# Half of the final modulation vector's steps on GpSimd, beside the output projection

## What is computed

```python
def _hybrid_mixer(...):
    ...
    return o @ w_o                      # the output projection

def reference(...):
    c_act = jax.nn.silu(c)
    ...
        x = x + g1 * _hybrid_mixer(h, ...)
        h = _modulate(_rmsnorm(x, norm2_gain[l]), sh2, sc2)
        x = x + g2 * _swiglu(h, w_gate[l], w_up[l], w_down[l])
    sh_f, sc_f = jnp.split(c_act @ w_mod_final + b_mod_final, 2, axis=-1)
    return _modulate(_rmsnorm(x, final_gain), sh_f, sc_f)
```

## Time and profile before

| | us |
|---|---|
| median of 3 runs | 1448.45 (1447.98 to 1451.27) |
| the profiled execution, whole | 1446.68 |
| the profiled execution, span from first to last instruction | 1445.0 |

### The profile page before, as it was taken

One profiled execution on the slowest core, in us unless ns is written; L12 is line 12 of the kernel. 1 busy time (PEld: TensorE's weight loads), 2 busy tenths in 40 slices (PEclk: granted clock), 3 DMA queues, 4 the chain that ended last, 5 costly groups with the idle time before them and its releaser, 6 DMA issues.

```text
span 1445.0 us, 18548 instructions
## 1 busy us (share of the span) xinstructions
PE 1341.7 (93%) x6181; PEld 1071.6 (74%) x6181; DVE 1023.3 (71%) x1468; ACT 684.6 (47%) x1157; POOL 727.8 (50%) x628
## 2 busy tenths in 40 slices
PE   2899999997899999989998899999999999999997
PEld 2668888785566666657876778888888888887886
DVE  4678699987877655554775986666666666378787
ACT  5456677736676655554125633223323334354332
POOL 3135444556677866652002165555555556578552
PEclk9899899998999999998999999999999999999999
DMA  9521234457534343312753244444444435989432
GB/s 326 178 62 30 88 126 135 144 162 203 131 76 114 88 125 116 89 43 84 272 172 114 88 152 155 167 168 167 168 158 146 146 141 197 362 296 327 150 109 117
DMA packets 123562, 220.20 MB, mean 152 GB/s; under 512 B 9386, under 2 KB 52500, under 8 KB 123220
## 3 DMA queue, kind: packets, MB, share of 16 engines
q1 hardware_dynamic: 123476, 219.12, 45.7%
HBM read 160.90 MB, written 57.93 MB: 151 GB/s over the span
## 4 chain that ended last, share of the span: by engine, by line
PE 41%; DVE 7%; issue 2%; DMA 1%; ACT 1%; POOL 0%; DVEq 0%; POOLq 0%; ACTq 0%
PE ps_out L2339 25%; PE ps_out L2365 12%; PE ps_out L1694 1%; DVE mod_acc_final L1759 1%; PE ps_out L1678 1%; DMA scr_mod_final<-mod_acc_final 1%; DVE y_full L1780 1%; DVE wgu_lo L2446 0%; PE ps_out L1702 0%; ACT square_junk L2257 0%; DVE x L2601 0%; DVE y_gated L1792 0%; DVE down_part L2599 0%; DVE h_sum_t L2413 0%; DVE h_t_full L2413 0%
## 5 line engine op out<-in xcount | busy, mean ns | idle before, releaser
L2036 POOL TENSOR_TENSOR wgu_lo<-wgu_raw,wgu_hi 128x512 fp32r<-128x512 f32 x66 | 97.4, 1483 | 127.6 <-ACT wgu_hi L2028 127.6
L2273 POOL TENSOR_TENSOR dn_lo<-dn_raw,dn_hi 128x512 fp32r<-128x512 f32 x77 | 126.9, 1665 | 67.1 <-ACT dn_hi L2179 67.0
L2028 ACT ACTIVATE wgu_hi<-wgu_sum 128x512 fp32r<-128x512 f32 x88 | 55.2, 632 | 199.7 <-DVE wgu_sum L2429 80.0
L2339 PE MATMUL ps_out<-h_b_t_hi,wgu_hi 128*128 128x512 f32 x352 | 138.1, 392 | 6.6 <-DVE h_b_t_lo L2417 2.6
L483 POOL TENSOR_TENSOR win_lo<-win_raw,win_hi 128x256 fp32r<-128x256 f32 (+1 forms) x84 | 66.7, 824 | 141.0 <-ACT win_hi L473 115.7
L2339 PE MATMUL ps_out<-h_b_t_hi,wgu_lo 128*128 128x512 f32 x352 | 137.7, 391 | 0.0
L2339 PE MATMUL ps_out<-h_b_t_lo,wgu_hi 128*128 128x512 f32 x352 | 137.5, 391 | 0.0
L2179 ACT ACTIVATE dn_hi<-dn_raw 128x1024 fp32r<-128x1024 f32 x77 | 81.2, 1062 | 114.4 <-PE ps_out L2365 55.7
L2365 PE MATMUL ps_out<-dn_hi 128*128 128x512 f32 x308 | 120.2, 390 | 0.0
L2365 PE MATMUL ps_out<-dn_hi,dn_lo 128*128 128x512 f32 x308 | 119.8, 389 | 0.0
L2365 PE MATMUL ps_out<-dn_lo,dn_hi 128*128 128x512 f32 x308 | 119.8, 389 | 0.0
(11 more groups left out here) (356 smaller groups left out, 3648.9 us busy)
## 6 DMA issues: line engine op xcount, KB each, us to landing
scr_act_sums<-act_sums SPq DMA_DIRECT2D x11, 1792.0 KB, 6.7
dn_raw<-scr_act_sums SPq DMA_DIRECT2D x77, 256.0 KB, 5.3
wmod_c<-in_w_mod_dram SPq DMA_DIRECT2D x48, 256.0 KB, 2.9
wgu_raw<-in_w_gate_dram SPq DMA_DIRECT2D x11, 1024.0 KB, 5.3
wgu_raw<-in_w_up_dram SPq DMA_DIRECT2D x11, 1024.0 KB, 5.4
wd_sums<-in_w_down_dram SPq DMA_DIRECT2D x11, 1024.0 KB, 4.8
scr_wd_sums<-wd_sums SPq DMA_DIRECT2D x11, 1024.0 KB, 4.1
dn_raw<-scr_wd_sums SPq DMA_DIRECT2D x44, 256.0 KB, 7.0
```

Of the source, the lines that this page charges most:

```text
L2036: pool.tensor_tensor(sl[slot(m, x)][:], src, sh[slot(m, x)][:].bitcast(F32), ALU.subtract).then_inc(wlp, 1)
L2273: pool.tensor_tensor(bl[q % NSLOT][:, 1], braw[entry(q)][:, 1], bh[q % NSLOT][:, 1].bitcast(F32), ALU.subtract).then_inc(dlw, 1)
L2339: last = pe.matmul(bank(m, b), a[s][:, t], h[x][t // 2][:, t % 2], start=(fresh and t == 0 and a is sh and h is hh), stop=(t == 3 and a is ...
```

## The change

The 32 steps are split by column group. VectorE keeps groups 0 and 1, 16 steps, two in each of tiles 0 to 7. GpSimd takes groups 2 and 3, also 16 steps, in a loop of its own between the 1/rms of the head groups (line 1644) and the 1/rms of row blocks 0 to 3 (line 1646). A GpSimd step is one multiplication for the first step of a group, and for the others a multiplication in place in the load buffer, a wait for it, and an addition to its own accumulator `fb`. Each side has two load buffers where there were four, in the same memory, and each has its own semaphores. In SyncE's queue the loads alternate: GpSimd's load of step f, then VectorE's load of step f, each waiting until its own step f - 2 is done. The two waits for all stores of the vector (64 of one semaphore) become waits for 32 of each of two, and one of ScalarE's waits gains a partner.

```diff
-    NFW = 4
+    fb = nc.alloc_sbuf_tensor_at("mod_acc_final_pool", [P, HALF], F32, offset=g.top - 14 * 1024)
+    NFW = 2
     fw = nc.alloc_sbuf_tensor_at("wmod_final", [P, NFW, HALF], F32, offset=g.top - 8 * 1024)
+    fx = nc.alloc_sbuf_tensor_at("wmod_final_pool", [P, NFW, HALF], F32, offset=g.top - 4 * 1024)
...
-    NF, FY = 4 * KD, 8
+    NF, FY = 2 * KD, 8
...
+        def load_final_pool(f):
+            c, t = f // KD, f % KD
+            if f >= NFW:
+                sp.wait_ge(fpa, f - NFW + 1)
+            if f >= KD and t == NFW - 1:
+                sp.dma_start(modf[:, half(2 + c - 1)], fb[:]).then_inc(fpo, 16)
+            sp.dma_start(fx[:, f % NFW], A["w_mod_final"][P * t:P * t + P, half(2 + c)]).then_inc(fxl[f % NFW], 16)
+
         for n in range(NY):
             for f in final_steps(n):
+                load_final_pool(f)
                 load_final(f)
             if n == FY:
                 sp.wait_ge(fmd, NF)
-                sp.dma_start(modf[:, half(3)], fa[:]).then_inc(fmo, 16)
+                sp.dma_start(modf[:, half(1)], fa[:]).then_inc(fmo, 16)
+                sp.wait_ge(fpa, NF)
+                sp.dma_start(modf[:, half(3)], fb[:]).then_inc(fpo, 16)
...
         pool.tensor_tensor(rc[:, NT:2 * NT], rc[:, NT:2 * NT], g.nhalf[:], ALU.pow).then_inc(rsd, 1)
+        for f in range(NF):
+            c, t = f // KD, f % KD
+            pool.wait_ge(fxl[f % NFW], 16 * (f // NFW + 1))
+            by = g.csil[:, t:t + 1].to_broadcast([P, HALF])
+            if t == 0:
+                if c:
+                    pool.wait_ge(fpo, 16 * c)
+                pool.tensor_tensor(fb[:], fx[:, f % NFW], by, ALU.mult).then_inc(fpa, 1)
+            else:
+                pool.tensor_tensor(fx[:, f % NFW], fx[:, f % NFW], by, ALU.mult).then_inc(fpr, 1)
+                pool.wait_ge(fpa, f)
+                pool.wait_ge(fpr, f - c)
+                pool.tensor_tensor(fb[:], fb[:], fx[:, f % NFW], ALU.add).then_inc(fpa, 1)
         pool.wait_ge(s2, 4)
...
-            act.wait_ge(p4.fmo, 64)
+            act.wait_ge(p4.fmo, 32)
+            act.wait_ge(p4.fpo, 32)
...
         act.wait_ge(p4.fmd, p4.NF)
+        act.wait_ge(p4.fpa, p4.NF)
```

More of the change, by code:

```diff
@@ L1551, in phase4 @@
     fmo = k.sem("mod_final_stored")
-    NF, FY = 4 * KD, 8
+    fxl = k.sems("wmod_final_pool_loaded", NFW)
+    fpr = k.sem("mod_final_pool_product")
+    fpa = k.sem("mod_final_pool_added")
+    fpo = k.sem("mod_final_pool_stored")
+    NF, FY = 2 * KD, 8
     STEP_T = {(1, 10): 0, (0, 10): 1, (1, 11): 2, (0, 11): 3, (1, 12): 4, (0, 12): 5, (1, 13): 6, (0, 13): 7}
@@ L1802, in phase4 @@
     p.yam, p.yfr, p.ysc, p.x1r, p.s2, p.rs2, p.fmd, p.fmo, p.ybm = yam, yfr, ysc, x1r, s2, rs2, fmd, fmo, ybm
+    p.fpa, p.fpo = fpa, fpo
     p.NY, p.NF = NY, NF
@@ L2139, in sync @@
                 sp.wait_ge(u2n, 4)
-                sp.wait_ge(p4.fmo, 64)
+                sp.wait_ge(p4.fmo, 32)
+                sp.wait_ge(p4.fpo, 32)
                 sp.dma_start(mfin[:], modf.rearrange("p (c n) -> p c n", c=4)).then_inc(mfl, 16)
```

## The result

The changed kernel takes 1451.45 us (median of 20 runs, 1448.7 to 1454.3), the kernel before, run beside it, 1447.77 us (median of 20, 1444.7 to 1451.27). The ratio is 1.0026, with a 95% interval from 1.0018 to 1.0035: 3.7 us slower, 0.26%. The profiled execution of the changed kernel took 1449.02 us with a span of 1447.3, against a span of 1445.0 before.

A forecast was written before the change was run, and what follows sets the result against it. It took the start of early_xhat, following VectorE's pace, to set the rest. A 5.9 us delay less 1.1 us from TensorE gave +4.8 us: 1453.2 us, 0.33% slower, range 1447.8 to 1458.5 for 8 in 10.

The forecast's parts named there:

- The start of early_xhat: VectorE's scaling after tile 7's work, which the feed-forward part hangs on: 756.0, 5.9 us later than 750.1.
- the walk: Working through the 16 projection steps across three engine streams with landings, queue and mutual waits: GpSimd's last step ends at 754.5.
- 4.9 of holding: Projection: VectorE and GpSimd instructions with SBUF operands wait for each other, 4.9 of the 5.9 us on early_xhat.
- 1.0 of loads: Projection: GpSimd's loads through two buffers and SyncE's queue, and the change of group, 1.0 of the 5.9 us.
- The hand-over of 0.14 us: Between VectorE and GpSimd: the waiting engine gets in 0.14 us before the other's running instruction ends.
- Rival 2: Projection: neither engine gets in before the other has quite ended; +11.4 - 1.1, so 1458.8 us; chance 0.08.
- rival 3: Projection: no holding between the engines, only the loads; +1.0 with no change of clock, 1449.4 us; chance 0.15.
- rival 4: Faster: GpSimd's last step ends before 748.7, early_xhat 3.0 us earlier than now, 1445.4 us; chance 0.08.
- rival 5: SyncE's queue starves both sides, loads behind stores land in 4.8 us; +10.3 - 1.1, 1457.7 us; chance 0.09.
- the row: Profile row for SyncE's loads in the projection: 3.8 us to land, the median of 28.
- What TensorE gives back: Around tile 10: longer idling moves the slow clock stretch, so tile 14's y_sb runs faster; -1.1 us, bounds 0 and -1.5.
- the term of the clock: TensorE's granted clock after its idle time ahead of the first transpose: -1.1 us in the sum.

The follow-up runs named there:

- e1: Changed kernel with each GpSimd multiplication and addition of the 16 steps replaced by two fills with zero, loads and waits kept: 1446.73 us, 0.9995 of the kernel before.
- e9: Changed kernel with GpSimd's loads issued by GpSimd itself, load f + 2 right after step f, in place of SyncE: 1454.44 us, 1.0043 of the kernel before.
- e4: Kernel before, all 32 steps on VectorE, with an accumulator for each of the four groups: 1444.1 us, 0.9969 of the kernel before.
- e5: Changed kernel with two accumulators a side, so neither engine waits for its first group's store: 1453.39 us, 1.0038 of the kernel before.
- e7: Changed kernel with two accumulators a side and the 1/rms of row blocks 0 to 3 ahead of GpSimd's steps 14 and 15: 1452.32 us, ratio 1.0035.
- e6: Changed kernel with GpSimd's two 1/rms instructions for row blocks 0 to 3 moved ahead of its steps 14 and 15: 1452.28 us, ratio 1.0038.

## Why the prediction came out as it did

*The start of early_xhat: right.* Forecast 57.2 us after tile 0 (5.9 later than before), measured 57.11 (5.84 later). It ended idle by GpSimd's 1/rms, as said. GpSimd's last step ended 55.69 us after tile 0 (forecast 754.5 - 698.85 = 55.65), VectorE's 54.6 (54.6), the store of GpSimd's first group left at 26.1 (26.6). The way there was off at two places, so the hit within 0.1 us is in part luck. The x addition of tile 7 ended at 49.65, not 51.15, because VectorE trailed less and then stood 2.73 us for its last load. And GpSimd's steps 9 and 11 ended at 33.65 and 40.16, where the walk had 35.15 and 42.15; then the load of step 12 stood in SyncE's queue behind the store of row block 2, which waits for VectorE's x addition of tile 5, and landed 4.75 us after its issue. The walk had given these steps 3.8 us and no such store. The two misses, some 2 us each, cancel: step 13 ended at 49.10 (49.05).

*What it is made of: right in the main.* 4.9 of holding and 1.0 of loads were 4.6 and 1.2 by e1. The means said the same: GpSimd's multiplications 1241 ns and additions 1508, 0.20 and 0.24 above 1.04 and 1.27 where I had said 0.25; steps of VectorE 1368 within 1.1 to 1.4; x additions 1082 and y_gated 895, less than the 1.1 I had given them; y_full 740. The hand-over of 0.14 us held too: the x addition that starts at 745.23 and takes 1.59 waits 0.90, so that it gets in at 746.13, and GpSimd's addition of 744.72 ends at 746.27. Rival 2, full exclusion to the end, falls by this and by its 11.4; rival 3, no holding, falls by these means and by e1; rival 4 needed GpSimd's last step at 748.7 or sooner, 49.85 after tile 0, and it ended at 55.69; rival 5 needed 4.8 us a landing, and the medians are 3.6 and 3.9.

*The loads of SyncE's queue.* At the Trainium skill's fit ("DMA: Bandwidth & Descriptors", section on the anatomy of one DMA), an estimate of 2.6 us for 256 KB, the forecast was +2.6 us and 1451.1. The 13 GpSimd loads issued from 700 to 751 took 3.6 at the median, so the trace decides for the row and not for the fit, which is for GpSimd's queue. In e9, where these loads are on that queue, they took 3.9 at the median too. The time by itself would have misled: 1451.45 is nearer to the 1451.1 than to the 1453.2 of the forecast.

*What TensorE gives back: the step that was mis-sized.* Forecast 1.1 us, bounds 0 and 1.5. Measured 5.84 - 3.97 = 1.87, above the upper bound. The mechanism was as written: 6.57 us idle ahead of the first transpose (6.6), a second wait of 0.77 (under 2), the slow stretch on y_d of tile 10, and y_sb of tile 14 at full clock. But the way from the second transpose to the next y_d went from 5.12 us (759.56 to 764.68) to 3.58 (763.39 to 766.97): 1.54, with the two transposes that I had left to the bound. The other 0.33 lies between early_xhat and that transpose; the kernel before had an idle 0.46 us ahead of its x addition of tile 8, which the changed kernel hasn't.

*The sum.* +4.8 forecast, +3.97 in the traces, +3.7 in the medians, 0.26%; with 20 runs a side the interval (1.0018 to 1.0035) does not reach 1. I had set the bound of what a measurement tells at 0.3% and gave more chance to the side above it (0.53) than below (0.39); the time came out below, by the term of the clock. With 1.87 in its place the sum is +4.0 us, 0.28%.

*What the prediction missed.* Its comparison was of the change with the kernel before. That the gain that VectorE could have, some 5 us, was to be had from the waits for the stores alone, with GpSimd left out of it (e4), was in rows that I had read and summed up as 7.3 us. And my expectations for e5 to e7 all fell: each took a wait away and I let the ones behind it move up, without asking which other wait lay under it.

## What to carry to other kernels

Before work is moved from VectorE to GpSimd, count on both engines the instructions that take two operands from SBUF: each pair that meets can cost each side up to most of the other's running instruction (here an x addition of 0.69 us became 1.59), so that VectorE, with 16 of 32 steps moved away, was busy 3.4 us longer. Look first for what else makes the engine trail; here separate accumulators in place of one that waits for its store brought 3.8 us and no contention. Where a buffer is freed late, several waits lie under each other: price the removal of one by the next one that ends, in the queue's own order.

## What the hardware showed that I had not expected

- A plain fill on GpSimd and VectorE's tensor_scalar of one SBUF tile by a column hold each other, though the two-operand steps are free beside fills: in e1 the tensor_scalar took 0.65 us at 727.40, not 0.48, and a fill 0.79 at 699.10, not 0.53. In the changed kernel that same instruction took 1.51 beside an addition. The "Who interferes with whom" section of "SBUF — State Buffer" in the Trainium skill names tensor_scalar among the operations that can take the shared ports whole, and the trace agrees.
- early_xhat, a tensor_scalar too, took 4.49 us for four instructions beside GpSimd's steps in e6, and 2.74 alone.
- A load issued by GpSimd costs it 0.58 us and a 0.30 wait ahead of it (e9), where SyncE mostly issues one in 0.33 to 0.46 (up to 1.42 behind the store of a row block in the changed kernel).
- A wait of TensorE of 2.0 us was followed by a fall of the granted clock in four of eleven traces (0.58 over 784 to 788 in e7) and by none in seven, the wait being the same to 0.01 us. Where it fell, it cost 1.6 us.
